# A two-block transformer on one core: where the gated rows of each expert are turned

## The chip, the cores and the metric

One core of a Trainium2 chip runs the whole program. The metric is device time in microseconds (us) of one execution. Everything is float32 outside; the large products run in three parts (below).

## The reference

The input has 512 tokens of 1024 features. The first block is an mLSTM and pooling mixer followed by a mixture of 32 experts, each token going to two of them. The second block (a gated spatial unit, a feed-forward net, differential attention, another feed-forward net) follows. The change touches the experts alone. Cut to what matters:

```
def run_block(args):                 # one expert e, up to 128 rows
    tok, e = args
    xb = hf[jnp.minimum(tok, n_tok - 1)]
    a = xb @ w_gate[e]               # 128x1024 @ 1024x512
    b = xb @ w_up[e]
    return (jax.nn.silu(a) * b) @ w_down[e]     # 128x512 @ 512x1024
```

## The kernel before, in words

**Split products.** A float32 number x is split into a rounded high part (fp32r) and a low part x - high. A product is three matmuls, high x high, high x low and low x high (`mm3`, L263 is the helper that issues each). So every weight has to be rounded on ScalarE (`Stream.high`, L191, raw to whi) and subtracted on VectorE (`Stream.low`, L210, wlo = raw - whi), in halves of 128x1024. SP loads the weights in items of 1 MB (`Stream.load`, L175) into four raw buffers, `raw0` to `raw3`; an item's buffer is free once its wlo is written. There are four places for whi and wlo too, and a place is free once the matmuls of its item are done.

**The experts.** The weights of all experts are one stream of items in a fixed order, six for each expert: two of the gate weights (`eg`), two of the *previous* expert's down weights (`ed`), two of the up weights (`eu`). `take_act` and `take_vec` round and subtract the items ahead by up to four, as far as places allow, so that each call waits for the item four before to be used up.

For expert n TensorE does, in `experts_pe`:
1. `rows_in_pe(eg)`: the first product, rows times gate weights, 24 matmuls (12 per item).
2. `rows_out_pe(n - 1)`: the down product of the expert before, 24 matmuls into two banks.
3. `rows_in_pe(eu)`: the second product, rows times up weights, 24 matmuls.
4. `turn_pe(n + 1)`: eight transposes (L1905) of the next expert's gathered rows, XN.
5. four transposes (L1955) of the gated rows GM of expert n, which wait for GM.

ScalarE copies the turned rows to XT's high part (L1972, `turn_act`), applies silu to the first product (L1997, SG), copies the down product out (L1988, YB) and copies the turned gated rows to GTh (L2011). VectorE multiplies SG by the second product (L2029, GM), writes XT's low part (L1979, `turn_vec`) and GT's low part (L2033, GTl). XT, SG and YB have two buffers each; GM and GT have one. GpSimd gathers the rows of an expert four ahead (L1841) and scatters its output (L1849).

**Order.** Each engine's order is written out by hand in `experts_pe`, `experts_act` and `experts_vec`. PSUM's eight banks go round in the order in which `R.plan` calls stand; `R.full` is "the matmuls into the bank are done", `R.done` "its reader is done", `R.claim` waits for the bank's reader before. One wait in VectorE's loop sets much of what follows: GM comes behind the roundings of the second product's calls, and XT's low part comes behind GM.

Of the kernel before, what the change touches and what calls it, by code (L numbers as in the profile page):

```python
# [7 lines left out]
F32 = mybir.dt.float32  # L8
# [3 lines left out]
ALU = mybir.AluOpType  # L12
ACT = mybir.ActivationFunctionType
AX = mybir.AxisListType.X

P = 128
# [4 lines left out]
NE = 32  # L21
# [211 lines left out]
def program(nc, g, out):  # L233
    ctx = ExitStack()
    with ctx:
# [4 lines left out]
        def sb(name, shape, dt=F32):  # L240
            t = scope[-1].enter_context(nc.sbuf_tensor(name, shape, dt))
            where[name] = nc.sbuf_base - math.prod(shape[1:]) * (2 if dt == BF16 else 4)
            return t
# [11 lines left out]
        S = Sems(nc, ctx)  # L255
        R = Ring(S, [ctx.enter_context(nc.psum_tensor(f"ps{i}", [P, 512], F32)) for i in range(8)])
        W = Stream(S)
# [7 lines left out]
        def mm3(e, o, l, r, start, stop):  # L265
            mm(e, o, l[0], r[0], start, False)
            mm(e, o, l[0], r[1], False, False)
            return mm(e, o, l[1], r[0], False, stop)
# [4 lines left out]
        ident = sb("ident", [P, P])  # L273
# [88 lines left out]
        GM = sb("GM", [P, DE])  # L362
        GTs = [sb("GTh", [P, TB, P], F32R), sb("GTl", [P, TB, P], F32R)]
# [128 lines left out]
        A_, V_ = "bank_act", "bank_vec"  # L492
# [73 lines left out]
        R.plan("tok", 1, V_)  # L566
        R.plan("x0", 2, V_)
        for n in range(NE):
            R.plan(f"eg{n}", 1, A_)
            W.mid(W.index[f"eg{n}"][0])  # L570
            W.ends[W.index[f"eg{n}"][1]] = R.full(f"eg{n}")
            if n > 0:
                R.plan(f"ey{n - 1}", 2, A_)
                W.mid(W.index[f"ed{n - 1}"][0])
                W.ends[W.index[f"ed{n - 1}"][1]] = R.full(f"ey{n - 1}", 1)
            R.plan(f"eu{n}", 1, V_)
            W.mid(W.index[f"eu{n}"][0])
            W.ends[W.index[f"eu{n}"][1]] = R.full(f"eu{n}")
            if n + 1 < NE:
                R.plan(f"x{n + 1}", 2, V_)  # L580
            if n == NWS:
                R.plan("ws", 2, A_)
            R.plan(f"et{n}", 1, V_)
        R.plan(f"ey{NE - 1}", 2, A_)
        W.mid(W.index[f"ed{NE - 1}"][0])
        W.ends[W.index[f"ed{NE - 1}"][1]] = R.full(f"ey{NE - 1}", 1)
# [1157 lines left out]
        def table_vec(e, own):  # L1744

            EJ = CJ[:, 36:68]
            n_of = CJ[0:1, 36:36 + NOVF].unsqueeze(2).broadcast_to([1, NOVF, 32])
            e.tensor_tensor(IE[:, :, :], NO[0:1, 1, :].unsqueeze(1).broadcast_to([1, NOVF, 32]), n_of, ALU.is_gt).then_inc(*own.up())
            e.tensor_tensor(IF_[:, :, :], NO[0:1, 2, :].unsqueeze(1).broadcast_to([1, NOVF, 32]), n_of, ALU.is_le).then_inc(*own.up())
            e.tensor_scalar(CV[:, 7:8], NO[0:1, 1, 31:32], -1.0, float(NOVF), ALU.mult, ALU.add).then_inc(*own.up())  # L1750
            e.wait_ge(*own.now())
            e.tensor_tensor(IE[:, :, :], IE[:, :, :], IF_[:, :, :], ALU.mult).then_inc(*own.up())
            e.wait_ge(*own.now())
            e.tensor_tensor(IE[:, :, :], IE[:, :, :], EJ[0:1, :].unsqueeze(1).broadcast_to([1, NOVF, 32]), ALU.mult).then_inc(*own.up())
            e.wait_ge(*own.now())
            e.tensor_reduce(CV[:, 0:NOVF], IE[:, :, :], AX, ALU.add).then_inc(*own.up())
            e.wait_ge(*own.now())
            e.tensor_copy(CT[:, :], CV[:, :]).then_inc(S("table"), 1)
# [126 lines left out]
        def gating_pe(e):  # L1885
            for q in range(2):
                b = R.claim(e, "ws", q)
                e.wait_ge(S("ws_masked"), q + 1)
                for k in range(4):
                    i = e.transpose(b[:, k * P:(k + 1) * P], WSN[q][:, k, :], ident[:, :])  # L1890
                i.then_inc(*R.fill("ws", q))
# [13 lines left out]
                    i = e.transpose(b[:, k * P:(k + 1) * P], XN[:, n % 4, kc * P:(kc + 1) * P], ident[:, :])  # L1905
                i.then_inc(*R.fill(f"x{n}", half))

        def rows_in_pe(e, n, name):
            b = R.claim(e, f"{name}{n}")
            for q, j in enumerate(W.index[f"{name}{n}"]):  # L1910
                w = W.parts(j)
                for k in range(4):
                    kc = 4 * q + k
                    if k % 2 == 0:
                        e.wait_ge(*W.half(j, k // 2))
                    if k == 0:
                        e.wait_ge(*R.done(f"x{n}", q))
                    i = mm3(e, b[:, :], [x[:, kc, :] for x in XT[n % 2]], [x[:, k, :] for x in w], kc == 0, kc == KC - 1)
                if q == 0:
                    i.then_inc(S("w_used"), 1)  # L1920
                else:
                    i.then_inc(*R.fill(f"{name}{n}"))

        def rows_out_pe(e, n):
            by = [R.claim(e, f"ey{n}", 0), R.claim(e, f"ey{n}", 1)]
# [15 lines left out]
        def experts_pe(e):  # L1941
            turn_pe(e, 0)
            for n in range(NE):
                rows_in_pe(e, n, "eg")
                if n > 0:
                    rows_out_pe(e, n - 1)
                rows_in_pe(e, n, "eu")
                if n + 1 < NE:
                    turn_pe(e, n + 1)
                if n == NWS:  # L1950
                    gating_pe(e)
                b = R.claim(e, f"et{n}")
                e.wait_ge(*R.done(f"eu{n}"))
                for k in range(4):
                    i = e.transpose(b[:, k * P:(k + 1) * P], GM[:, k * P:(k + 1) * P], ident[:, :])  # L1955
                i.then_inc(*R.fill(f"et{n}"))
            rows_out_pe(e, NE - 1)

        def take_act(e, name):
            for j in W.index[name]:  # L1960
                W.high(e, j + W.depth(j))

        def take_vec(e, name):
            for j in W.index[name]:
                W.low(e, j + W.depth(j))

        def turn_act(e, n):
            if n >= 2:
                e.wait_ge(*R.full(f"eu{n - 2}"))
            for half in range(2):  # L1970
                e.wait_ge(*R.full(f"x{n}", half))
                e.activation(XT[n % 2][0][:, 4 * half:4 * half + 4, :],  # L1972
                             R.bank(f"x{n}", half)[:, :].rearrange("p (c n) -> p c n", c=4), ACT.Copy).then_inc(S("xt_hi"), 1)
# [15 lines left out]

        def experts_act(e, own):  # L1990
            turn_act(e, 0)
            for n in range(NE):
                take_act(e, f"eg{n}")
                if n >= 2:
                    e.wait_ge(*R.done(f"eu{n - 2}"))
                e.wait_ge(*R.full(f"eg{n}"))
                e.activation(SG[n % 2][:, :], R.bank(f"eg{n}")[:, :], ACT.Silu).then_inc(*R.free(f"eg{n}"))  # L1997
                if n > 0:
                    take_act(e, f"ed{n - 1}")
                    out_act(e, own, n - 1)  # L2000
                take_act(e, f"eu{n}")
                if n + 1 < NE:
                    turn_act(e, n + 1)
                if n == 2:
                    gating_loads_act(e)
                if n == NWS:
                    gating_act(e)
                if n > 0:
                    e.wait_ge(*R.full(f"ey{n - 1}", 1))
                e.wait_ge(*R.full(f"et{n}"))  # L2010
                e.activation(GTs[0][:, :, :], R.bank(f"et{n}")[:, :].rearrange("p (c n) -> p c n", c=4),  # L2011
                             ACT.Copy).then_inc(S("gt_hi"), 1)
            take_act(e, f"ed{NE - 1}")
            out_act(e, own, NE - 1)

        def experts_vec(e, own):
            W.low(e, W.index["eg0"][1] + 1)
            turn_vec(e, 0)
            table_vec(e, own)
            for n in range(NE):  # L2020
                take_vec(e, f"eg{n}")
                if n > 0:
                    take_vec(e, f"ed{n - 1}")
                take_vec(e, f"eu{n}")
                e.wait_ge(*R.done(f"eg{n}"))
                e.wait_ge(*R.full(f"eu{n}"))
                if n > 0:
                    e.wait_ge(*R.full(f"et{n - 1}"))
                e.tensor_tensor(GM[:, :], SG[n % 2][:, :], R.bank(f"eu{n}")[:, :], ALU.mult).then_inc(*R.free(f"eu{n}"))  # L2029
                if n + 1 < NE:  # L2030
                    turn_vec(e, n + 1)
                e.wait_ge(S("gt_hi"), n + 1)
                e.tensor_tensor(GTs[1][:, :, :], R.bank(f"et{n}")[:, :].rearrange("p (c n) -> p c n", c=4),  # L2033
                                GTs[0][:, :, :].bitcast(F32), ALU.subtract).then_inc(*R.free(f"et{n}"))
            take_vec(e, f"ed{NE - 1}")


# [998 lines left out]
```

## Time and profile before

| | |
|---|---|
| median of 3 runs | 2106.32 us (2103.11 to 2106.4) |
| the profiled execution | 2103.96 us |
| its span | 2102.2 us |
| TensorE busy | 1973.2 us (94%) |
| VectorE busy | 1186.1 us (56%) |
| ScalarE busy | 968.8 us (46%) |
| GpSimd busy | 187.3 us (9%) |
| mean granted clock of TensorE | 0.978 |

The span is the time from the first to the last instruction of the profiled execution; the execution's own time is 1.8 us more. The experts run from about 290 to 900 us of it. "PEld" is TensorE's loading of the stationary operand, which runs beside the matmuls. A matmul's duration of 389 ns is longer than the distance to the next, 0.23 us, because they overlap in the array: distances between starts are what counts on TensorE.

### The profile page before, as it was taken

What the parts mean: (1) busy time and instruction counts of PE and PEld (TensorE: products, weight loads), DVE (VectorE), ACT (ScalarE), POOL (GpSimd) and SP (SyncE); (2) the same over time, 40 slices, a digit from 0 to 9 for tenths busy, and PEclk for the clock granted to TensorE, in tenths of its full rate; (3) what the DMA queues carried; (4) which work ended last, traced back from release to release, by engine and by line L of the source; (5) the groups of instructions that cost most, each with busy time, mean ns of one, the idle gap of its engine ahead of it and who ended that gap; (6) DMA issues with size and microseconds to landing.
All of it is one profiled execution on the core that took longest, in us unless ns stands there. A gap on an engine that the chain in (4) does not pass through costs nothing.

```text
span 2102.2 us, 22854 instructions
## 1 busy us (share of the span) xinstructions
PE 1973.2 (94%) x8918; PEld 1580.7 (75%) x8918; DVE 1186.1 (56%) x1536; ACT 968.8 (46%) x1467; POOL 187.3 (9%) x245
## 2 busy tenths in 40 slices
PE   4999988999999999979999999998999979999997
PEld 3757857777777777748888888886777768888886
DVE  6675588888888888843543333335345443333322
ACT  3433157787778878734332222224355442222221
POOL 3100111103111010020000000000011100000000
PEclk8999889999999999989999999999999999999999
DMA  8444379999999999942223223222111114323210
GB/s 280 140 156 166 110 235 353 343 350 367 354 358 344 338 340 349 343 156 81 88 86 105 90 93 101 90 90 83 61 61 61 61 46 145 100 83 103 96 41 40
DMA packets 195578, 361.88 MB, mean 172 GB/s; under 512 B 13398, under 2 KB 79707, under 8 KB 195468
## 3 DMA queue, kind: packets, MB, share of 16 engines
q1 hardware_dynamic: 179522, 337.67, 46.6%
q10 hardware_dynamic: 5818, 11.98, 1.6%
q0 software_dynamic: 10128, 10.73, 1.5%
q8 instruction: 73, 1.20, 0.2%
q14 instruction: 37, 0.30, 0.0%
HBM read 364.52 MB, written 20.97 MB: 183 GB/s over the span
## 4 chain that ended last, share of the span: by engine, by line
PE 86%; DVE 7%; DMA 3%; issue 2%; ACT 1%; SPq 1%; POOL 0%; ACTq 0%; DVEq 0%; POOLq 0%
PE ps L263 84%; DVE wlo L210 3%; DMA raw<-in_w_in 1%; DMA raw<-in_w_expert_down 1%; PE ps L1955 1%; DVE GM L2029 1%; PE ps L725 1%; SPq L880 1%; ACT whi L191 0%; PE ps L2509 0%; DVE hT5l L260 0%; DVE X L839 0%; ACT XN L683 0%; PE ps L1172 0%; DVE hT4l L763 0%
## 5 line engine op out<-in xcount | busy, mean ns | idle before, releaser
L210 DVE TENSOR_TENSOR wlo<-raw,whi 128x1024 fp32r<-128x1024 f32 (+1 forms) x576 | 671.4, 1216 | 323.7 <-ACT whi L191 320.7
L191 ACT ACTIVATE whi<-raw 128x1024 fp32r<-128x1024 f32 (+1 forms) x576 | 573.0, 1047 | 237.0 <-PE ps L263 216.5
L263 PE MATMUL ps<-hT5h,whi 128*128 128x512 f32 x352 | 137.8, 391 | 6.3 <-DVE wlo L210 6.3
L263 PE MATMUL ps<-hT5l,whi 128*128 128x512 f32 x352 | 137.6, 391 | 0.0
L263 PE MATMUL ps<-hT3h,whi 128*128 128x512 f32 x352 | 137.0, 389 | 0.6 <-DVE hT3l L260 0.6
L263 PE MATMUL ps<-hT5h,wlo 128*128 128x512 f32 x352 | 137.4, 390 | 0.0
L263 PE MATMUL ps<-hT3l,whi 128*128 128x512 f32 x352 | 136.9, 389 | 0.0
L263 PE MATMUL ps<-hT3h,wlo 128*128 128x512 f32 x352 | 136.9, 389 | 0.0
L2372 DVE TENSOR_TENSOR tmpT<-tmpT,ps 128x512 f32<-128x512 f32 x44 | 30.1, 684 | 139.6 <-PE ps L263 139.6
L263 PE MATMUL ps<-whi,XT0h 128*128 128x512 f32 x256 | 102.3, 400 | 0.6 <-DVE XT0l L1979 0.6
L263 PE MATMUL ps<-whi,GTh 128*128 128x512 f32 x256 | 99.7, 389 | 1.7 <-DVE GTl L2033 1.7
L263 PE MATMUL ps<-whi,XT1h 128*128 128x512 f32 x256 | 101.0, 394 | 0.0
L263 PE MATMUL ps<-whi,XT0l 128*128 128x512 f32 x256 | 100.8, 394 | 0.0
L263 PE MATMUL ps<-wlo,XT0h 128*128 128x512 f32 x256 | 100.6, 393 | 0.0
L263 PE MATMUL ps<-whi,XT1l 128*128 128x512 f32 x256 | 99.7, 390 | 0.0
L263 PE MATMUL ps<-wlo,XT1h 128*128 128x512 f32 x256 | 99.7, 389 | 0.0
L263 PE MATMUL ps<-wlo,GTh 128*128 128x512 f32 x256 | 99.6, 389 | 0.0
L263 PE MATMUL ps<-whi,GTl 128*128 128x512 f32 x256 | 99.6, 389 | 0.0
L688 POOL TENSOR_SCALAR small<-small 128x1 f32<-128x1 f32 x32 | 13.2, 411 | 956.7 <-ACT XN L683 897.6
L839 DVE TENSOR_TENSOR X<-X,ps 128x512 f32<-128x512 f32 x64 | 43.3, 685 | 92.1 <-PE ps L263 92.1
L2347 ACT ACTIVATE tmpT<-ps 128x512 f32<-128x512 f32 x44 | 26.4, 600 | 134.8 <-PE ps L263 133.1
L263 PEld LDWEIGHTS ps<-hT5h,whi 128*128 128x128 f32 x352 | 66.5, 189 | 20.3 <-issue 6.5
(432 smaller groups left out, 4064.8 us busy)
## 6 DMA issues: line engine op xcount, KB each, us to landing
raw<-in_w_expert_gate SPq DMA_DIRECT2D x64, 1024.0 KB, 7.3
raw<-in_w_expert_up SPq DMA_DIRECT2D x64, 1024.0 KB, 8.1
raw<-in_w_expert_down SPq DMA_DIRECT2D x64, 1024.0 KB, 6.7
raw<-in_ffn_w_gu SPq DMA_DIRECT2D x44, 1024.0 KB, 5.1
raw<-in_ffn_w_down SPq DMA_DIRECT2D x20, 1024.0 KB, 5.1
raw<-in_ada_w SPq DMA_DIRECT2D x24, 512.0 KB, 4.7
raw<-in_w_in SPq DMA_DIRECT2D x8, 1024.0 KB, 5.9
raw<-in_a_w_in SPq DMA_DIRECT2D x8, 1024.0 KB, 6.0
```

Source lines behind the costliest of these rows:

```text
L191: e.activation(hi[:, c], raw[:, c], ACT.Copy).then_inc(self.S("w_hi"), 1)
L210: e.tensor_tensor(lo[:, c], raw[:, c], hi[:, c].bitcast(F32), ALU.subtract).then_inc(self.S("w_lo"), 1)
L263: return e.matmul(o, l, r, start=start, stop=stop, skip_group_check=True)
L688: e.tensor_scalar(out_, x, EPS, None, ALU.add).then_inc(*own.up())
L725: i = e.transpose(b[:, tb * P:(tb + 1) * P], XN[:, tb, kc * P:(kc + 1) * P], ident[:, :])
L839: e.tensor_tensor(X[:, tb, hs], X[:, tb, hs], R.bank(*name)[:, :], ALU.add).then_inc(*R.free(*name))
L880: e.dma_start(EARLY[n].rearrange("p (c n) -> p c n", c=2), ada_w[:, 2 * c:2 * c + 2, j * D:(j + 1) * D]).then_inc(S(f"early{n}"), 16)
L1955: i = e.transpose(b[:, k * P:(k + 1) * P], GM[:, k * P:(k + 1) * P], ident[:, :])
L2029: e.tensor_tensor(GM[:, :], SG[n % 2][:, :], R.bank(f"eu{n}")[:, :], ALU.mult).then_inc(*R.free(f"eu{n}"))
L2347: e.activation(tmpT[k][:, :], R.bank(f"fg{l}.{ng}", k)[:, :], ACT.Silu).then_inc(*R.free(f"fg{l}.{ng}", k))
L2372: e.tensor_tensor(tmpT[k][:, :], tmpT[k][:, :], R.bank(f"fu{l}.{ng}", k)[:, :], ALU.mult).then_inc(*R.free(f"fu{l}.{ng}", k))
```

## The change

In each expert but the first, the four transposes of the previous expert's gated rows now stand inside the first product, between the 12 matmuls of its first item and the 12 of its second (`turn_gated_pe`, called through `between`). On ScalarE the copy GTh stands between the two `take_act` calls of the gate weights, on VectorE the subtraction GTl between the two `take_vec` calls. The last expert's gated rows are turned behind the loop, as before. The bank of `et` is planned before that of `eg`, so that the count of filled banks keeps TensorE's order.

```
@@ the plan of the banks
         for n in range(NE):
+            if n > 0:
+                R.plan(f"et{n - 1}", 1, V_)
             R.plan(f"eg{n}", 1, A_)
...
-            R.plan(f"et{n}", 1, V_)
+        R.plan(f"et{NE - 1}", 1, V_)
@@ TensorE
-        def rows_in_pe(e, n, name):
+        def rows_in_pe(e, n, name, between=None):
...
                 if q == 0:
                     i.then_inc(S("w_used"), 1)
+                    if between is not None:
+                        between()
...
+        def turn_gated_pe(e, n):
+            b = R.claim(e, f"et{n}")
+            e.wait_ge(*R.done(f"eu{n}"))
+            for k in range(4):
+                i = e.transpose(b[:, k * P:(k + 1) * P], GM[:, k * P:(k + 1) * P], ident[:, :])
+            i.then_inc(*R.fill(f"et{n}"))
...
-                rows_in_pe(e, n, "eg")
+                rows_in_pe(e, n, "eg", (lambda: turn_gated_pe(e, n - 1)) if n > 0 else None)
@@ ScalarE (gated is the old wait and copy to GTh, unchanged)
-                take_act(e, f"eg{n}")
+                take_act(e, f"eg{n}", 0)
+                if n > 0:
+                    gated(n - 1)
+                take_act(e, f"eg{n}", 1)
@@ VectorE (gated is the old wait and subtraction to GTl, unchanged)
-                take_vec(e, f"eg{n}")
+                take_vec(e, f"eg{n}", 0)
+                if n > 0:
+                    gated(n - 1)
+                take_vec(e, f"eg{n}", 1)
```

ScalarE's order between two experts, before (`XT1h` is the high part of the next expert's turned rows, `whi<-raw` the rounding of half a weight item, `SG` the silu of the first product):

```order
L1972 ACTIVATE XT1h<-ps 128x512 x2
L2011 ACTIVATE GTh<-ps 128x512
L191 ACTIVATE whi<-raw 128x1024 x4
L1997 ACTIVATE SG<-ps 128x512
L191 ACTIVATE whi<-raw 128x1024 x4
```

and the same place with the change, buffer numbers shown:

```order
L1980 ACTIVATE XT1h<-ps0 128x512
L1980 ACTIVATE XT1h<-ps2 128x512
L191 ACTIVATE whi3<-raw3 128x1024 x2
L2005 ACTIVATE GTh<-ps3 128x512
L191 ACTIVATE whi0<-raw0 128x1024 x2
L2016 ACTIVATE SG1<-ps1 128x512
L191 ACTIVATE whi1<-raw1 128x1024 x2
```

The copy GTh has moved behind the first of the two items rounded there.

VectorE's order between two experts, before (`GM` is the gated rows, `XT1l` and `GTl` low parts):

```order
L210 TENSOR_TENSOR wlo<-raw,whi 128x1024 x12
L2029 TENSOR_TENSOR GM<-SG,ps 128x512
L1979 TENSOR_TENSOR XT1l<-ps,XT1h 128x512 x2
L2033 TENSOR_TENSOR GTl<-ps,GTh 128x512
```

and with the change:

```order
L2052 TENSOR_TENSOR GM<-SG1,ps3 128x512
L1987 TENSOR_TENSOR XT0l<-ps1,XT0h 128x512
L1987 TENSOR_TENSOR XT0l<-ps4,XT0h 128x512
L210 TENSOR_TENSOR wlo1<-raw1,whi1 128x1024 x2
L2037 TENSOR_TENSOR GTl<-ps5,GTh 128x512
L210 TENSOR_TENSOR wlo2<-raw2,whi2 128x1024 x2
```

GTl has moved behind the subtraction of one item; what stands in front of GM and of XT's low part is the same.

## Rows read from the trace of the kernel before

**Rows 1.** The page, busy time of each engine over the span.
```profile
span 2102.2 us, 22854 instructions
PE 1973.2 (94%) x8918; PEld 1580.7 (75%) x8918; DVE 1186.1 (56%) x1536; ACT 968.8 (46%) x1467; POOL 187.3 (9%) x245
```

**Rows 2.** Busy time by stretch: us, engines (x instructions), granted clock, DMA share, GB/s.
```profile
380.00:880.00 500.00, 479.83 (x2239) 392.93 (x2238) 439.31 (x427) 400.37 (x480) 64.13 (x60) 1.00 0.98 350
358.00:364.00 6.00, 2.18 (x14) 1.68 (x12) 5.14 (x5) 4.59 (x6) 1.02 (x1) 1.00 1.00 366
364.00:366.00 2.00, 1.68 (x6) 1.53 (x7) 1.37 (x3) 0.55 (x2) 0.00 (x0) 0.60 1.19 391
```

**Rows 3.** Waits from 380 to 880 us: who for whom, us, times, longest.
```profile
PE ps L1955 <- DVE GM L2029: 20.2, 26, 1.3
ACT whi L191 <- DMA raw<-in_w_expert_down: 3.6, 7, 0.9
```

**Rows 4.** Chain of waits, 560 to 700 us: start, us, what; one period and a stall.
```profile
592.22 16.59 PE ps L263 x72
...
608.85 0.78 DVE wlo L210
609.63 0.61 DVE GM L2029
...
611.00 2.97 PE ps L263 x12
...
617.54 7.78 DMA raw<-in_w_expert_down
```

**Rows 5.** TensorE's timeline between two experts: start, us, instruction, idle time before.
```profile
608.64 1.03 PE L1905 MATMUL ps<-ident,XN 128*128 128x128 f32 x8
610.38 0.63 PE L1955 MATMUL ps<-ident,GM 128*128 128x128 f32 x4 [0.70 <-DVE GM L2029]
610.98 0.47 PE L263 MATMUL ps<-whi,XT1h 128*128 128x512 f32 x1
```

**Rows 6.** VectorE's timeline there.
```profile
604.98 4.66 DVE L210 TENSOR_TENSOR wlo<-raw,whi 128x1024 fp32r<-128x1024 f32 x4 [0.75 <-ACT whi L191]
610.14 1.28 DVE L1979 TENSOR_TENSOR XT1l<-ps,XT1h 128x512 fp32r<-128x512 f32 x2
611.73 0.69 DVE L2033 TENSOR_TENSOR GTl<-ps,GTh 128x512 fp32r<-128x512 f32 x1 [0.30 <-ACT GTh L2011]
```

**Rows 7.** Line L1979 (XTl), 380 to 880 us, who waited for it (us, times).
```profile
L1979 DVE TENSOR_TENSOR XT1l<-ps,XT1h x28: 672/681/685, 384.3 to 874.8; 128x512 fp32r<-128x512 f32 x28
...
  PEld ps L263: 4.7, 26
```

**Rows 8.** ScalarE's timeline there.
```profile
603.40 0.60 ACT L1988 ACTIVATE YB<-ps 128x512 f32<-128x512 f32 x1 [0.17 <-PE ps L263]
603.89 2.00 ACT L191 ACTIVATE whi<-raw 128x1024 fp32r<-128x1024 f32 x2
...
611.10 0.60 ACT L2011 ACTIVATE GTh<-ps 128x512 fp32r<-128x512 f32 x1 [0.68 <-PE ps L1955]
611.59 2.00 ACT L191 ACTIVATE whi<-raw 128x1024 fp32r<-128x1024 f32 x2
614.06 2.01 ACT L191 ACTIVATE whi<-raw 128x1024 fp32r<-128x1024 f32 x2 [0.46 <-PE ps L263]
616.78 0.60 ACT L1997 ACTIVATE SG<-ps 128x512 f32<-128x512 f32 x1 [0.71 <-PE ps L263]
```

**Rows 9.** TensorE's timeline at 243 us: transposes between wide matmuls.
```profile
243.34 1.04 PE L1172 MATMUL ps<-ident,X 128*128 128x128 f32 x8
244.14 0.48 PE L263 MATMUL ps<-whi,hT1h 128*128 128x512 f32 x1
244.45 0.39 PE L263 MATMUL ps<-wlo,hT1h 128*128 128x512 f32 x1
```

**Rows 10.** Chain of waits: an expert's first matmuls after the gated rows were turned.
```profile
305.21 16.57 PE ps L263 x72
...
365.36 17.58 PE ps L263 x72
...
875.08 16.55 PE ps L263 x72
```

**Rows 11.** Line L1905, 380 to 880 us: min/median/max ns.
```profile
L1905 PE MATMUL ps<-ident,XN x216: 270/272/273, 382.8 to 873.5; 128*128 128x128 f32 x108
```

More of the change, by code:

```diff
@@ L1951, in experts_pe, with take_act, take_vec @@
                     gating_pe(e)
[L1952 to L1956, printed above, removed]
+            turn_gated_pe(e, NE - 1)
             rows_out_pe(e, NE - 1)
-        def take_act(e, name):
-            for j in W.index[name]:
+        def take_act(e, name, i=None):
+            for j in W.index[name] if i is None else [W.index[name][i]]:
                 W.high(e, j + W.depth(j))
-        def take_vec(e, name):
-            for j in W.index[name]:
+        def take_vec(e, name, i=None):
+            for j in W.index[name] if i is None else [W.index[name][i]]:
                 W.low(e, j + W.depth(j))
@@ L1991, in experts_act, with gated @@
             turn_act(e, 0)
+            def gated(n):
+                if n > 0:
+                    e.wait_ge(*R.full(f"ey{n - 1}", 1))
+                e.wait_ge(*R.full(f"et{n}"))
+                e.activation(GTs[0][:, :, :], R.bank(f"et{n}")[:, :].rearrange("p (c n) -> p c n", c=4),
+                             ACT.Copy).then_inc(S("gt_hi"), 1)
             for n in range(NE):
-                take_act(e, f"eg{n}")
+                take_act(e, f"eg{n}", 0)
+                if n > 0:
+                    gated(n - 1)
+                take_act(e, f"eg{n}", 1)
                 if n >= 2:
@@ L2007, in experts_act @@
                     gating_act(e)
[L2008 to L2012, printed above, removed]
+            gated(NE - 1)
             take_act(e, f"ed{NE - 1}")
@@ L2019, in experts_vec, with gated @@
             table_vec(e, own)
+            def gated(n):
+                e.wait_ge(S("gt_hi"), n + 1)
+                e.tensor_tensor(GTs[1][:, :, :], R.bank(f"et{n}")[:, :].rearrange("p (c n) -> p c n", c=4),
+                                GTs[0][:, :, :].bitcast(F32), ALU.subtract).then_inc(*R.free(f"et{n}"))
             for n in range(NE):
-                take_vec(e, f"eg{n}")
+                take_vec(e, f"eg{n}", 0)
+                if n > 0:
+                    gated(n - 1)
+                take_vec(e, f"eg{n}", 1)
                 if n > 0:
@@ L2031, in experts_vec @@
                     turn_vec(e, n + 1)
-                e.wait_ge(S("gt_hi"), n + 1)
-                e.tensor_tensor(GTs[1][:, :, :], R.bank(f"et{n}")[:, :].rearrange("p (c n) -> p c n", c=4),
-                                GTs[0][:, :, :].bitcast(F32), ALU.subtract).then_inc(*R.free(f"et{n}"))
+            gated(NE - 1)
             take_vec(e, f"ed{NE - 1}")
```

## Prediction

> **What bounds the kernel now.** The page comes first. The span is 2102.2 us and TensorE is busy for 94% of it, against 56% for VectorE and 46% for ScalarE [rows 1]. So a change matters if it changes how long TensorE takes per expert, and I went to the stretch of the experts.
>
> The stretch from 380 to 880 us has 480 of 500 us of TensorE busy at a granted clock of 1.00, and the DMA engines at a share of 0.98 [rows 2]. Two things are therefore nearly full at once. The waits of the same stretch say which of them TensorE meets. It waited 20.2 us in 26 pieces at the turning of the gated rows for GM (0.8 us an expert), while ScalarE waited for a down-projection transfer 7 times, 3.6 us in all [rows 3]. So the transfers are close behind but rarely last.
>
> The chain of waits shows one expert's period. From 592.22, 72 matmuls take 16.59 us. Then the chain goes through the last part of a weight rounding on VectorE (to 609.63) and GM (to 610.24), and the gated rows are turned [rows 4]. The next expert starts at 610.98 [rows 5], so an undisturbed period is 610.98 - 592.22 = 18.76 us; I use 18.78. It is tempting to stop here and call the wait for GM the bound. It is half of the story, and TensorE's own timeline tells the other half.
>
> After the eight row transposes (608.64 to 609.67) TensorE idles 0.70 us, turns GM's four pieces, and starts the next expert's first product at 610.98 [rows 5]. That product reads XTl, and VectorE writes XTl right behind GM: two pieces from 610.14 in 1.28 us, so the first half is there at about 610.8 [rows 6]. The weight loads of the products waited for exactly this write in 26 of 26 experts, 4.7 us together, 0.18 us each, **after** the gated rows had been turned [rows 7]. So two chains end at the same moment, and the four transposes fill time in which TensorE would have waited for XTl anyway.
>
> Where does the XTl chain begin? At the end of the down product (rows out). ScalarE's second YB copy starts at 603.40 when that product is complete, the rounding behind it at 603.89, VectorE's four roundings run from 604.98 without a gap into GM, then XTl [rows 6, 8]. From 603.4 to 610.98 it is 7.6 us, and TensorE's own work in it (24 matmuls and eight transposes) ends 1.3 us earlier. **The period is the time from an expert's start to the end of the down product in it, plus this fixed 7.6 us.** What is put before the end of the down product lengthens the period. What is taken from behind it gives nothing.
>
> **The change, part by part.**
> - *Removed between experts:* the wait for GM and four transposes, on 31 of 32 experts. TensorE's first product still needs XTl, and nothing the change moves stands in front of XTl: the same YB copies, roundings and GM come first on both engines. Gain 0 to 0.03 us each. Taken: 0. The cover is TensorE's idle time before XTl, which grows from 0.70 to about 1.3 us (609.67 to 610.98).
> - *Added in the middle of the first product:* four transposes, which find GM finished 3.5 us before (610.24 against 610.98 + 2.97 = 613.95 [rows 4]), so no wait. Their price: eight transposes between wide matmuls hold the next matmul from 243.34 to 244.14, that is 0.10 us each, and the first matmul after them takes 0.31 us to the next instead of 0.23 [rows 9]. Four cost 4 x 0.10 + 0.09 = 0.49 us. Bounds: 0.40 if the slower first matmul costs nothing, 0.63 as the four stand in the timeline today with idle time around them [rows 5]. All of it lies before the end of the down product, so it is on the path. 31 x 0.49 = 15.2 us.
> - *ScalarE and VectorE:* the copy GTh (0.60 us) and the subtraction GTl (0.69) move behind the first rounding. That rounding can start right after XT's copies, about 1.2 us earlier than 611.59 [rows 8]. The second one, today at 614.06, now stands behind GTh. The transposes end at about 614.4 and the copy at 615.1, so it starts about 0.9 us later. Queued behind it are the expert's gate activation (today 616.78 [rows 8], 0.5 us later now by itself) and VectorE's roundings, which reach the down product's end with the time they had. GTl is done at about 615.8, while the down product, its reader, starts at 610.98 + 24 x 0.23 + 0.49 = 617.0: hidden, with 1.2 us to spare. Cost 0.
> - *SP and GpSimd:* no issue is added or moved. The raw buffers come free 1.2 us earlier (first rounding) and 0.9 us later (second). This changes only when transfers are issued.
> - *Transfer stalls come back.* From 305.21 to 875.08 there are 30 periods, 569.9 us; at 18.78 they would be 563.4 [rows 10]. Of the 6.5 us over, 3.8 lie in the three periods to 365.36, where ScalarE also loads the next block's constants and the queue is overfull. Outside them a period averages (875.08 - 365.36) / 27 = 18.88 us, of which the DMA engines are busy 0.98, 18.5 us [rows 2, 10]. A period of 18.78 leaves them 0.3 us, one of 19.27 leaves 0.8. I give back most of the late 2.7 us and 0.5 us of the early 3.8, 2.6 us in all (bounds 0 and 6.5).
>
> The sum is 15.2 - 2.6 = +12.6 us. The profiled execution took 2103.96 us, so 2116.6; the median of the three runs, 2106.32, stands 2.4 above it and would give 2118.9. I take **2118**.
>
> One rule of the Trainium skill bears on the price. The trace has 272 ns for a transpose's own duration, but a pitch of 100 ns [rows 9, 11]. TensorE: Matmul & The Clock Gate (PE-mode transpose) gives about 275 ns for one in a kernel's context, most of it access latency. The trace agrees with the duration; charged in full it would make four 1.1 us, an estimate from the page, and the sum 31 x 1.1 - 2.6 = +31 us.
>
> **The rivals.**
> 1. *The wait for GM was the bound* (faster). If TensorE's release at 610.98 hung on the gated rows and XTl came early enough, the 0.70 us of idle and the 0.63 of transposes go and 0.49 comes back: 0.84 saved, until the transfers stop it at 18.5 us a period, 0.3 under today's mean of 19.0. 31 x 0.32 = 10: 2096. It decides if XTl is ready before about 609.8. For it speaks that the chain names GM in every expert; against it [rows 7]. Trainium skill, Perfetto Trace Analysis (Optimization Strategy): find the gaps of the contended engine and make what it waits for come sooner. Followed with the wait list alone, it gives this rival.
> 2. *The transfers set the pace anyway* (no change). Share 0.98 speaks for it. Then 0.49 us more of TensorE is absorbed and the time is 2106. Against it: 7 waits where it would need one in each expert.
> 3. *A transfer comes late* (slower still). The later second rounding frees its buffer about 0.9 us later. Its load, 7.78 us from issue to landing in the chain [rows 4], is the one ScalarE sometimes waits for, and its reader moves only 0.5. If that latency does not shrink, 0.4 us more in each period: 31 x 0.4 = 12, 2130.
> 4. *The clock drops* in the longer idle piece. After an idle piece in 358 to 364 us (2.18 of 6 us busy) the granted clock was 0.60 for 2 us [rows 2], the lower level of 1.2 GHz in part, and that expert's matmuls were about 1 us slower. Once in each expert that is +31: 2149. The new idle of 1.3 us is well short of that one (3.8 us of 6).
>
> **How the numbers follow.** My forecast has 0.76: its own range is 2110 (31 x 0.40 - 6.5 on 2103.96) to 2126 (31 x 0.63 on 2106.32). Rival 1 has 0.09, rival 2 0.07, rival 3 0.05, rival 4 0.03. The 8-in-10 range, 2108 to 2127, leaves out rivals 1 and 4 and part of 2 and 3. A measurement here can tell about 0.2%, 4.2 us. Faster 0.09; within 0.2% 0.08 (rival 2 and the edge of the forecast); slower 0.83.
>
> **What would show it.** Right: GM no longer among TensorE's waits; in its place a wait for XTl in each expert; 1.3 us from the end of the eight transposes to the next matmul, as before; the four transposes inside the first product at a pitch of 0.10; the undisturbed period 19.2 to 19.3; DMA share near 0.96; ScalarE's waits for transfers nearly gone. Wrong: a period under 18.8, or an XTl that lands earlier against the down product's end; or ScalarE waiting for transfers in most experts (rival 3).

## Result, and the profile after

| | before | changed |
|---|---|---|
| median of 6 runs each, same chip | 2102.69 us | 2120.68 us |
| ratio | | 1.0088, 95% interval 1.0063 to 1.0113 |
| the profiled execution | 2103.96 us | 2121.51 us |
| its span | 2102.2 us | 2119.8 us |
| undisturbed period of an expert | 18.78 us | 19.26 us |

The change made the kernel slower, by 13 to 24 us by its interval. A later comparison of the same two kernels (below) gave 1.0063, 1.0047 to 1.008, 10 to 17 us. The forecast was 2118 with a range of 2108 to 2127.

The page's busy times, to be read against [rows 1]: every engine does the work it did, in a longer span.

```profile
span 2119.8 us, 22854 instructions
PE 1975.8 (93%) x8918; PEld 1582.7 (75%) x8918; DVE 1184.3 (56%) x1536; ACT 965.0 (46%) x1467; POOL 185.7 (9%) x245
```

TensorE's timeline at the two places, one expert of the changed kernel (line 1907 turns the rows, 1932 the gated rows), against [rows 5]:

```profile
617.43 1.03 PE L1907 MATMUL ps<-ident,XN 128*128 128x128 f32 x8
619.76 0.47 PE L263 MATMUL ps<-whi,XT1h 128*128 128x512 f32 x1 [1.30 <-DVE XT1l L1987]
622.59 0.60 PE L1932 MATMUL ps<-ident,GM 128*128 128x128 f32 x4
```

Between experts the wait is now one piece of 1.30 us and its releaser is XTl. From the end of the eight transposes to the next matmul it is 619.76 - 618.46 = 1.30 us, as before (609.67 to 610.98). The four transposes in the middle have no idle time in front of them.

The chain of waits over the same expert, against [rows 4]:

```profile
603.93 13.67 PE ps L263 x60
617.60 0.04 DVEq L2051
617.64 0.78 DVE wlo L210
618.42 0.60 DVE GM L2052
619.02 0.61 DVE XT1l L1987
619.63 0.14 issue
619.76 2.98 PE ps L263 x12
622.75 0.44 PE ps L1932 x4
623.18 13.67 PE ps L263 x60
```

It is the chain of before with XTl in the place of the turning, and with a new piece of 0.44 us in the middle of the first product. From 600.49, the expert's start, to 619.76 it is 19.27 us.

The waits from 380 to 880 us (who for whom, us in total, times, longest), against [rows 3]:

```profile
ACT GTh L2005 <- PE ps L1932: 58.8, 26, 4.5
...
DVE GTl L2037 <- ACT GTh L2005: 36.7, 26, 3.0
...
PE ps L263 <- DVE XT0l L1987: 17.7, 13, 2.0
PE ps L263 <- DVE XT1l L1987: 15.9, 12, 1.6
...
ACT whi L191 <- DMA raw<-in_w_expert_down: 1.0, 1, 1.0
```

GM is gone from TensorE's waits and XTl has taken its place, with 33.6 us (17.7 + 15.9) where GM had 20.2. ScalarE waits for a down transfer once instead of 7 times. ScalarE and VectorE now stand idle for the turned rows, 58.8 and 36.7 us, and nothing on TensorE waits for that. Over the same stretch the DMA share is 0.96, as forecast.

### The profile page after: what moved, and what is told of

Its sections match the earlier page's. It is cut to its first block, busy times and chain, and to the rows that moved or that the text cites. A ratio compares the mean times of both kernels' runs of the same rounds, so it can differ in the third digit from the quotient of the medians.

```text
span 2119.8 us, 22854 instructions
## 1 busy us (share of the span) xinstructions
PE 1975.8 (93%) x8918; PEld 1582.7 (75%) x8918; DVE 1184.3 (56%) x1536; ACT 965.0 (46%) x1467; POOL 185.7 (9%) x245
## 4 chain that ended last, share of the span: by engine, by line
PE 86%; DVE 7%; DMA 2%; issue 2%; ACT 1%; SPq 1%; POOL 0%; ACTq 0%; DVEq 0%; POOLq 0%
PE ps L263 84%; DVE wlo L210 2%; DMA raw<-in_w_in 1%; DVE GM L2052 1%; DMA raw<-in_w_expert_down 1%; PE ps L1932 1%; SPq L882 1%; PE ps L727 1%; DVE XT0l L1987 0%; DVE XT1l L1987 0%; PE ps L2530 0%; DVE hT5l L260 0%; ACT whi L191 0%; DVE X L841 0%; PE ps L1174 0%
## 5 line engine op out<-in xcount | busy, mean ns | idle before, releaser
L690 POOL TENSOR_SCALAR small<-small 128x1 f32<-128x1 f32 x32 | 13.2, 412 | 954.1 <-ACT XN L685 895.8
L263 PEld LDWEIGHTS ps<-hT5h,whi 128*128 128x128 f32 x352 | 66.5, 189 | 20.2 <-issue 6.5
```

The lines of the kernel that those rows point to most:

```text
L263: return e.matmul(o, l, r, start=start, stop=stop, skip_group_check=True)
L690: e.tensor_scalar(out_, x, EPS, None, ALU.add).then_inc(*own.up())
```

## Experiments

All were compared with the kernel before on the same chip. "Period" is the distance of two experts' starts in an undisturbed part of the profile.

### XTl in front of GM, in the changed kernel

```
                 take_vec(e, f"eu{n}")
+                if n + 1 < NE:
+                    turn_vec(e, n + 1)
                 e.wait_ge(*R.done(f"eg{n}"))
...
                 e.tensor_tensor(GM[:, :], ...)
-                if n + 1 < NE:
-                    turn_vec(e, n + 1)
```

(The bank of `eu` is released on a semaphore of its own, so that the counts keep their order. The next run needs it too.)

> The changed kernel with VectorE's XTl put in front of GM. Theory (the chain from the down product through YB, four roundings, GM and XTl sets the period): XTl no longer waits for GM (0.60 us) but for XT's high part, which is copied 0.3 us after the last rounding, so the next expert starts about 0.2 us sooner; undisturbed period 19.05 instead of 19.26, about 6 us less than the changed kernel in all. Rival (the place of XTl on VectorE doesn't matter, TensorE's own work sets the period): 19.26, no difference.

Measured: ratio 1.0044 (1.0026 to 1.0063), 2113.89 us; period 633.14 - 614.04 = 19.10. The chain of waits:

```profile
612.57 0.61 ACT XT1h L1980
613.18 0.02 issue
613.20 0.70 DVE XT1l L1987
613.90 0.14 issue
614.04 3.00 PE ps L263 x12
```

GM and the last rounding have left the chain. TensorE starts 0.86 us after XT's high part arrives. Moving two VectorE instructions, with TensorE's order untouched, shortened every undisturbed expert by 0.16 us. The gain is read from the period; the time alone does not show it, since its interval overlaps the one of the second comparison of the changed kernel.

### XTl in front of GM, in the kernel before

The same edit without the change.

> The kernel before with XTl in front of GM. Theory of two chains that end together: now GM and with it the turning of the gated rows come later by the two XTl pieces and their wait for XT's high part, 1.5 us, and since the turning stands between experts, TensorE waits for all of it: period 20.3 instead of 18.78, about 45 us slower than before. If only XTl counted there, it would get 0 to 0.2 us per expert faster.

Measured: ratio 1.0252 (1.0212 to 1.0291), 2157.28 us; period 630.69 - 610.49 = 20.20. The chain of waits:

```profile
627.40 0.61 ACT XT1h L1972
628.64 0.68 DVE XT1l L1979
629.32 0.61 DVE GM L2031
630.06 0.63 PE ps L1955 x4
```

With GM moved back, TensorE waits for all of it, at the turning between experts. Bringing XTl forward costs 1.4 us an expert there, while in the changed kernel the same edit is a gain. Together with the changed kernel, where taking GM's wait away left the wait for XTl, this says that before the change two chains ended together.

Not all of the 54 us comes from that 1.4. TensorE idles 2.32 us before the turning in nearly every expert, and 7 of the 31 experts after the first began at a lower clock, with periods of 21.3 to 21.8 us. The 30 periods from expert 1 to expert 31 take 616.1 us, 10 more than 30 x 20.20. One of these starts, 446 to 449 us (busy time of the engines, clock 0.56, DMA share, GB/s):

```profile
446.00:449.00 3.00, 3.00 (x11) 2.46 (x10) 1.38 (x2) 2.26 (x3) 0.00 (x0) 0.56 0.98 336
```

### The copies back in front of the first rounding

```
-                take_act(e, f"eg{n}", 0)
                 if n > 0:
                     gated(n - 1)
-                take_act(e, f"eg{n}", 1)
+                take_act(e, f"eg{n}")
```

and the same on VectorE.

> The changed kernel with the copies GTh and GTl back in front of the first rounding on ScalarE and VectorE; only TensorE's transposes stay in the middle of the first product. It prices the placement of the copies, which the prediction put at nothing. Theory: ScalarE now stands before GTh until 3.5 us into the product with all roundings queued behind it; the eight roundings on VectorE then run on without idle into GM and XTl; period 20.6 to 20.9 against 19.26, some 45 us slower than the changed kernel. Rival (the roundings have slack, only the transposes count): 19.26.

Measured: ratio 1.0564 (1.0537 to 1.0592), 2224.61 us. The best period is as expected (551.76 to 572.37, 20.61), but most are 21 to 24.7 us. ScalarE's timeline in one of them:

```profile
575.91 0.60 ACT L2005 ACTIVATE GTh<-ps 128x512 fp32r<-128x512 f32 x1 [5.36 <-PE ps L1932]
576.40 3.89 ACT L191 ACTIVATE whi<-raw 128x1024 fp32r<-128x1024 f32 x4
580.20 0.58 ACT L2015 ACTIVATE SG<-ps 128x512 f32<-128x512 f32 x1
580.67 3.90 ACT L191 ACTIVATE whi<-raw 128x1024 fp32r<-128x1024 f32 x4
...
589.25 2.00 ACT L191 ACTIVATE whi<-raw 128x1024 fp32r<-128x1024 f32 x2 [1.81 <-DMA raw<-in_w_expert_down]
```

ScalarE stands 5.4 us before GTh and then works through a pile of roundings. From 380 to 880 us it waits for a down transfer 22 times, 34.6 us in all, against once and 1.0 us in the changed kernel; that the transfers are late because the buffers come free late is my reading and was not tested apart. TensorE's idle pieces between experts are 1.7 to 4.4 us long, and 21 of the 31 experts after the first began at a lower clock. I expected the pile alone, and with it less than half of the loss. That the copies cost nothing in the change holds for their place behind the first rounding, and not for the one in front of it.

### The four transposes twice in the middle

```
-            for k in range(4):
+            for k in (0, 1, 2, 3, 0, 1, 2, 3) if n < NE - 1 else (0, 1, 2, 3):
```

> The changed kernel with the four transposes of the gated rows done twice in the middle of the first product, the second time over the first (30 experts). It prices four transposes on the path. Theory: 4 x 0.10 = 0.40 us more per expert, period 19.66 against 19.26, about 12 us slower than the changed kernel. Rival (in the middle they cost what they cost between experts, 0.63, or nothing because something else ends later): 19.9 or 19.26.

Measured: ratio 1.0137 (1.0106 to 1.0168), 2128.58 us. The chain of waits:

```profile
600.80 13.65 PE ps L263 x60
614.45 0.04 DVEq L2051
614.48 0.78 DVE wlo L210
615.26 0.60 DVE GM L2052
615.86 0.61 DVE XT1l L1987
616.47 0.14 issue
616.61 3.00 PE ps L263 x12
619.61 0.87 PE ps L1932 x8
```

Period 636.30 - 616.61 = 19.69. Four more transposes cost 0.43 us, and nothing else in the chain moved.

### Turned at the old place too

The last argument leaves out the semaphore, so nobody waits for these four.

```
+                if n + 1 < NE:
+                    turn_gated_pe(e, n, False)
             turn_gated_pe(e, NE - 1)
```

> The changed kernel, and the gated rows are also turned at their old place between experts, into the same bank, with nobody waiting for it. TensorE's idle time before XTl is then broken up as before the change. Theory: the undisturbed period stays at 19.26, since those transposes fill idle time; the fall of the granted clock in the first expert after the long idle piece (first 12 matmuls 4.18 us instead of 2.99) goes away, and the kernel is 1.6 to 4 us faster than the changed kernel. Rival A (transposes between experts do cost): period 19.7. Rival B (the clock falls for another reason): the first 12 matmuls stay at about 4.2 us.

Measured: ratio 1.0081 (1.0063 to 1.0099), 2117.77 us; period 631.65 - 612.38 = 19.27. Four transposes between experts cost nothing, the same four in the middle of the product 0.48 us. TensorE's timeline at expert 1 (the experts count from 0; the expectations call it the first) has them in what was one idle piece of 1.9 us:

```profile
299.47 0.63 PE L1932 MATMUL ps<-ident,GM 128*128 128x128 f32 x4 [1.33 <-DVE GM L2055]
300.07 0.47 PE L263 MATMUL ps<-whi,XT1h 128*128 128x512 f32 x1
```

The first item of this expert (its first 12 matmuls) took 2.95 us instead of 4.18, and the one after the constants' loads still 4.55, behind an idle piece of 2.17 and the four transposes. The first of these proves little: with the transposes doubled, that item took 3.01 us too, after an idle piece of 1.92. The gain of 1.6 to 4 us that I expected is not told apart from none: the ratio lies inside the interval of the changed kernel's first comparison and within 0.2% of the second.

### The constants' loads apart

In expert 2 ScalarE issues four loads for the next block. Here they are issued in experts 2, 4, 6 and 9.

```
-                if n == 2:
-                    gating_loads_act(e)
+                if n in (2, 4, 6, 9):
+                    gating_loads_act(e, n)
```

> The changed kernel with the four loads of constants, which ScalarE issues in one piece in expert 2, issued in experts 2, 4, 6 and 9. Theory (the disturbed periods come from those loads: they overfill the transfers, TensorE idles longer, and then its clock falls): the two periods from 326.33 to 367.37 us shrink from 41.0 to 38.5 us and the slow first 12 matmuls after them (4.58 us) go back to 3.0: about 4 us less than the changed kernel. Rival (the disturbance is left over from the start of the expert stage): no difference.

Measured: ratio 1.0039 (1.002 to 1.0058), 2114.98 us. The stretch went as expected: the two periods from 326.33 to 364.90 take 38.6 us, and the next first item 3.01. But this profile has a disturbance elsewhere, at an expert whose down transfer was 0.84 us late, where TensorE idled 1.86 us and the first item took 4.42. And expert 1 began slowly here too, after an idle piece of 1.96 us.

### Both edits together, and the changed kernel again

> Turned twice and the constants' loads apart together: the changed kernel without its disturbances. Theory: from expert 1 to expert 31 the 30 periods take 578 to 580 us (30 x 19.27), against 586.3 in the changed kernel and 569.9 before; no first item of an expert slower than 3.0 us; about 8 us less than the changed kernel, so 9 to 11 us over the kernel before. Rival (the disturbances move to other experts): 583 or more, and the time as with one of the two edits.

> The changed kernel again, on the same chip as the run beside it, for the comparison: 15 to 21 us over the kernel before; the slow first items (over 4 us) in the first expert and after the constants' loads again.

Measured: together 1.0044 (1.003 to 1.0058), 2112.84 us; the changed kernel again 1.0063 (1.0047 to 1.008), 2117.66 us. With both edits the 30 periods run from 298.84 to 877.34, 578.5 us, and no first item takes over 2.99. That is 30 x 19.28: the undisturbed loss by itself. The time is 9.3 us over the kernel before by its ratio (6.3 to 12.2). In the changed kernel's second profile the 30 periods take 585.2 us. The slow first item after the loads is there (5.46 us, after an idle piece of 3.88). The one in expert 1 is not (3.01), though TensorE had idled 1.91 us before it, as in the first profile. So that one comes and goes, and the second expectation missed it.

### Only the rows turned in the middle

The kernel before, with the turning of the next expert's rows moved into the second product on all three engines:

```
-                rows_in_pe(e, n, "eu")
-                if n + 1 < NE:
-                    turn_pe(e, n + 1)
+                rows_in_pe(e, n, "eu", (lambda: turn_pe(e, n + 1)) if n + 1 < NE else None)
...
-                take_vec(e, f"eu{n}")
+                take_vec(e, f"eu{n}", 0)
+                if n + 1 < NE:
+                    turn_vec(e, n + 1)
+                take_vec(e, f"eu{n}", 1)
```

and the same on ScalarE; the banks of `x` are planned before that of `eu`.

> The kernel before with only the next expert's rows turned in the middle of the second product; the gated rows are turned between experts as before. Theory: XTl is early, but it pushes VectorE's last rounding and GM back by about 2 us, and the gated rows, turned between experts, wait for GM: period about 20.8, some 60 us slower than before. Rival (XTl's chain alone was the bound before): faster than before by up to 0.2 us per expert.

Measured: ratio 1.0224 (1.0191 to 1.0257), 2151.28 us; undisturbed period 614.50 - 594.53 = 19.97. Slower, as expected, and 0.8 us less per expert than expected. The mechanism is the expected one: XTl is early, and the turning of the gated rows between experts waits for GM.

```profile
613.13 0.61 DVE GM L2033
613.74 0.14 issue
613.88 0.63 PE ps L1955 x4
```

Here too a part of the loss of 48 us is the clock: with an idle piece of 2.08 us in nearly every expert, 10 of 31 began at a lower one.

### Both turned in the middle

The changed kernel with that edit.

> The changed kernel, and the next expert's rows are turned in the middle of the second product too, with XT's copies between the roundings on ScalarE and VectorE. Theory: neither GM nor XTl is waited for between experts any more; TensorE's own work is 16.6 + 8 x 0.10 + 4 x 0.10 + 0.3 = 18.1 us, below the 18.5 us that the transfers need, so the transfers or VectorE (16.6 us of work per expert) set the period: 18.5 to 18.7, time about 2092 to 2100, faster than both. Rival (the transposes themselves are the whole loss and the place of XTl gives nothing): about 19.2, as the changed kernel.

Measured: ratio 0.9873 (0.9837 to 0.991), 2074.99 us, faster than I had thought possible. The chain of waits in an undisturbed part:

```profile
641.08 0.87 PE ps L1907 x8
641.95 5.47 PE ps L263 x24
647.43 0.44 PE ps L1932 x4
647.86 10.94 PE ps L263 x48
658.80 0.87 PE ps L1907 x8
```

TensorE waits for nothing: 5.47 + 0.44 + 10.94 + 0.87 = 17.72 us a period. And the transfers follow. Busy time from 380 to 480 us, against [rows 2]:

```profile
380.00:480.00 100.00, 100.00 (x476) 83.15 (x475) 93.28 (x90) 84.92 (x103) 26.93 (x22) 1.00 1.03 377
```

Where I had read a DMA share of 0.98 as nearly full, the same engines move 377 GB/s here for 100 us. The limit is near: ScalarE waits for a gate or up transfer 34 times from 380 to 880 us, 19.3 us in all.

### Both in the middle, and the loads apart

> The kernel with both sets of transposes inside the products, and the constants' loads apart as in the run beside it. There TensorE idles 2.8 us before 357.49 and the transfers are nearly full. Theory: about 3 us less than with the loads together, 2072, the fastest of all. Rival (transfers are so full that the same bytes cost the same wherever they stand): the waits only spread over experts 4 to 9, 2075.

Measured: ratio 0.9824 (0.9802 to 0.9845), 2071.4 us, the fastest of all. The direction was as expected. Whether the loads made it is open: the intervals of this run and the one above overlap, and the two profiled spans stand the other way round (2075.4 and 2070.3 us). The profiles speak for the rival: the 30 periods take 540.1 us with the loads apart against 539.0 with them together, the idle piece of 2.8 us before 357.49 is gone, and periods of 17.9 to 20.0 us stand from 392 to 522 us in its place.

## Why the prediction was right

**The mechanism.** The prediction said that the period runs from an expert's start to the end of the down product in it, and from there over YB, four roundings, GM and XTl. It said that the wait for GM, though the chain named it in every expert, covered a second wait that ended at the same moment. Three runs show it from three sides. The transposes at the old place are free (turned twice, 19.27 against 19.26). XTl in front of GM is a gain in the changed kernel and a loss in the one before. And moving the gated rows alone or the rows alone loses, while both together win 28 us: each of two waits hid behind the other.

**The price of the four transposes** was 0.49 us, taken from eight transposes elsewhere (the rows give 0.08 for the slower first matmul, where the sum has 0.09). Measured: 19.26 - 18.78 = 0.48, of which 0.44 is the row in the chain; the doubled ones cost 0.43. By the duration of one, 272 ns in the trace, it would have been 1.1. The Trainium skill, TensorE: Matmul & The Clock Gate (PE-mode transpose), gives about 275 ns for it; the trace agrees with that duration, and what counted here was the pitch.

**The copies** cost nothing where they stand, and the margins were as worked out. The subtraction GTl is done at 624.6; the down product, its reader, starts 12 matmuls after 623.18, at about 625.9. The second rounding moved back (from 3.1 to 4.0 us after the expert's start) without TensorE waiting for it.

```profile
623.91 0.69 DVE L2037 TENSOR_TENSOR GTl<-ps,GTh 128x512 fp32r<-128x512 f32 x1 [1.37 <-ACT GTh L2005]
```

**What came back from stalls** is the term that was wrong in sum. I gave back 2.6 us. From expert 1's start to expert 31's the changed profile has 586.3 us (305.48 to 891.77) against 569.9 [rows 10], 16.4 more. 30 x 0.48 = 14.4 of it are the transposes, so the disturbances grew by 2.0 instead of shrinking (by 0.9 in the second profile, 585.2 us): the term has the wrong sign, and is off by 3.5 to 4.6 us. They fall into two parts. The waits for late transfers, which are what is left when the slow pieces are taken off, shrank from about 5.1 to 3.8 us. But three experts (305.48, 367.37, 832.41) began at a lower clock. Their first item took 4.18, 4.58 and 4.58 us instead of 3.0, and the transposes behind the first of them 0.83 instead of 0.44, some 4.7 us in all, where before one expert was about 1 us slower [rows 10] and the four transposes in front of it took 1.03 us instead of 0.63.

The granted clock in two microseconds soon after each of these starts (window, us, busy time of the engines, clock, DMA share, GB/s):

```profile
306.00:308.00 2.00, 2.00 (x8) 1.63 (x7) 2.00 (x2) 0.14 (x1) 0.00 (x0) 0.73 1.01 372
368.00:370.00 2.00, 2.00 (x7) 1.60 (x6) 2.00 (x2) 0.00 (x0) 0.00 (x0) 0.59 1.03 354
834.00:836.00 2.00, 2.00 (x6) 1.53 (x5) 1.12 (x1) 0.00 (x0) 0.00 (x0) 0.50 0.93 354
```

and what TensorE did before the last of them:

```profile
832.41 0.60 PE L263 MATMUL ps<-whi,XT0h 128*128 128x512 f32 x1 [2.00 <-DVE XT0l L1987]
```

This is the fourth rival, which I had as happening in every expert or in none. With the transposes gone from between experts, an idle piece of 1.2 to 1.4 us there, as it comes whenever anything is late, is 1.9 to 2.0, and the clock then fell to its 1.2 GHz level for a while in some profiles and not in others. The regular 1.30 us never brought it down. That the missing transposes are the cause is likely and not shown (last section). So the term belonged in the sum, for the disturbed experts. The one at 832.41 also shows what remains of rival 3: its chain comes from a down transfer of 7.64 us, the one that ScalarE waited for. The run with both edits, which has hardly a disturbance left, is 9.3 us over the kernel before, near 30 x 0.48 less the stalls that are gone: 14.4 - 6.5 = 7.9. That run also moves the loads, which the kernel before does not, so it prices the change without its disturbances and not the change alone.

**The rivals.** Rival 1 (GM was the bound) is refuted: from expert 1 on no period of the changed kernel was under 19.2. Its price was also worked out wrongly, with 18.5 us as the least period that the transfers allow; the run with both in the middle has 17.72. And the sum took 0.3 us for the distance from 18.5 to the mean of 19.0, which is 0.5. Rival 2 (the transfers set the pace) falls by the same run. The share of 0.98 that spoke for it was demand, not a ceiling. The Trainium skill, DMA: Bandwidth & Descriptors (Where 436 GB/s comes from), gives about 358 GB/s as what HBM allows one core, and says that this binds for transfers from HBM; the trace does not agree, with 377 GB/s over 100 us. The same section names a measurement of 425 GB/s, and the trace is consistent with that one. Rival 3 (a transfer comes late) is not seen as a cost of every period: from 380 to 880 us ScalarE waited for a down transfer once. It is seen where the copies stand too early.

**The size.** The sum of +12.6 us stands against +18.5 (13.2 to 23.8) and, in the second comparison, +13.3 (9.9 to 16.8). The profile has +17.6 in the span. That 2118 came so close to 2120.68 is partly luck. I took the sum from a base that the later runs put lower (2106.32, then 2102.69), and on the later base the same sum gives 2115.3: the base made up for about half of what the sum was short.

## To carry to other kernels

A chain of waits names what ended last, not what ended second. Before an instruction is moved away from a wait, look at what the next instruction behind it waits for; here one row (XTl, 0.18 us in every expert) showed that the gap would stay, and that two things had to move together. What fills an idle piece is free and what is put into a busy stretch has its full pitch, even when it is the same instruction. A DMA share near 1 is no bound by itself as long as nobody waits for a transfer.

## What the hardware showed that I had not expected

- The DMA engines moved 350 GB/s at a share of 0.98 [rows 2] and 377 GB/s at 1.03 over 100 us. The share had hardly room left, and the rate still rose by 8%.
- The length of the idle piece between two experts does not settle whether the granted clock falls. After unbroken pieces of 1.86 to 2.00 us it fell four times (1.86, 1.92, 1.96, 2.00) and stayed three times (1.91, 1.92, 1.95). It fell after 3.25 and 3.88 us in the changed kernel and after 2.78 with XTl in front, stayed after 2.53 with the transposes doubled, and stayed after several of 2.4 to 3.5 with the copies in front. Where a long piece came in every expert, it fell in 7 of 31 (2.32 us in most, then four transposes) and in 10 of 31 (2.08 us in most, then four transposes). It never fell after the regular 1.30.
- Whether four short transposes inside such a piece keep the clock up stays open. In the kernel before and in the two runs that turn twice, pieces of 1.23 to 1.44 us with the transposes behind them came seven times and the clock stayed up each time, where the unbroken pieces of about the same whole length brought it down in four of seven. But after 2.17 us and four transposes it fell too.
- Fp32 transposes of 128x128 follow each other at 0.10 us though each lasts 0.27, and the first wide matmul after them is 0.08 us slower than the next ones.
